# Delta rule in a two-block forward pass: steps 10 to 22 of each head moved by one slot

## The reference, cut to what matters

```
proj = h @ w_in                                   # q, k, v, z of the delta rule; q x3, k, v, z of the attention
qkv  = silu(causal_depthwise_conv(concat(aq, ak, av), conv_w))
a_strict = where(strict, beta * (k @ k.T) * decay, 0)
sol  = triangular_solve(a_strict, [v * beta, k * beta * exp(g)], unit_diagonal=True)   # u, w
v_new = u - w @ state
o     = (q * exp(g)) @ state + (q @ k.T * decay) @ v_new
state = state * exp(g_last) + (k * exp(g_last - g)).T @ v_new
```

## Time and profile before

| what | value |
|---|---|
| median of 3 runs | 2958.02 us (2957.57 to 2958.8) |
| profiled execution | 2963.54 us, its span 2961.7 us |
| mean granted TensorE clock | 0.994 of full speed |
| busy: TensorE, VectorE, ScalarE, GpSimd | 97%, 73%, 50%, 15% of the span |
| instructions | 50340 |

### The profile page before, as it was taken

How to read it: one execution, slowest core, us unless ns; L and a number is a source line. 1 busy time by engine, 2 the same in 40 slices (tenths; PEclk the granted TensorE clock), 3 DMA queues, 4 the chain that set the end, 5 groups by cost and what they waited for, 6 DMA issues and landing times.

```text
span 2961.7 us, 50340 instructions
## 1 busy us (share of the span) xinstructions
PE 2881.1 (97%) x16934; PEld 2502.1 (84%) x16934; DVE 2167.7 (73%) x3182; ACT 1480.9 (50%) x2124; POOL 454.5 (15%) x188
## 2 busy tenths in 40 slices
PE   7999999999999999999999999999999999999998
PEld 6888888888888888888887787788888888888887
DVE  6677777777679888888877998976787437465456
ACT  4454444454344444444445777765544444444443
POOL 0111101111000000000000000000003435545443
PEclk9999999999999999999999999999999999999999
DMA  6544444554568888788875455466684666767655
GB/s 220 169 148 152 157 149 158 161 160 168 159 205 297 306 300 317 289 298 317 302 255 186 164 171 171 164 206 221 230 324 157 198 206 229 252 227 242 205 185 178
DMA packets 199089, 636.93 MB, mean 215 GB/s; under 512 B 32312, under 2 KB 46776, under 8 KB 198208
## 3 DMA queue, kind: packets, MB, share of 16 engines
q1 hardware_dynamic: 165024, 601.92, 58.6%
q10 hardware_dynamic: 33952, 33.52, 3.6%
HBM read 619.61 MB, written 15.75 MB: 215 GB/s over the span
## 4 chain that ended last, share of the span: by engine, by line
PE 75%; DVE 10%; issue 6%; ACT 5%; DMA 3%; ACTq 0%; DVEq 0%; SPq 0%; POOL 0%; POOLq 0%
PE gemm L552 46%; PE gemm L557 23%; DVE wl L1569 3%; ACT wh L1008 3%; DMA Em<-E_scratch 2%; PE side L896 1%; DVE dT L1759 1%; DVE dW L1757 1%; DMA raw<-in_stream 0%; PE side L878 0%; DMA E_scratch<-dA 0%; PE side L578 0%; DVE xs L1658 0%; DVE ny L1644 0%; DVE t L2180 0%
## 5 line engine op out<-in xcount | busy, mean ns | idle before, releaser
L552 PE MATMUL gemm<-xs,wh 128*128 128x512 f32 x5120 | 1624.9, 399 | 28.9 <-DVE stage L1574 8.1
L1008 ACT ACTIVATE wh<-raw 128x1024 fp32r<-128x1024 f32 x939 | 983.2, 1058 | 949.1 <-PE gemm L557 816.2
L1569 DVE TENSOR_TENSOR wl<-raw,wh 128x1024 fp32r<-128x1024 f32 x811 | 1033.1, 1279 | 459.1 <-ACT wh L1008 436.9
L557 PEld LDWEIGHTS gemm<-xs,wl 128*128 128x128 f32 x5120 | 964.1, 188 | 215.8
L557 PE MATMUL gemm<-xs,wl 128*128 128x256 f32 x5120 | 1013.6, 279 | 0.0
L552 PEld LDWEIGHTS gemm<-xs,wh 128*128 128x128 f32 x5120 | 780.1, 189 | 60.6 <-issue 44.1
L552 PE MATMUL gemm<-hid,wh 128*128 128x512 f32 x2368 | 745.0, 396 | 8.9 <-DVE xacc L1601 2.3
L557 PEld LDWEIGHTS gemm<-hid,wl 128*128 128x128 f32 x2368 | 445.1, 188 | 101.3
L557 PE MATMUL gemm<-hid,wl 128*128 128x256 f32 x2368 | 467.4, 279 | 0.0
L1497 POOL TENSOR_TENSOR wl<-raw,wh 128x1024 fp32r<-128x1024 f32 x128 | 350.2, 2741 | 364.7 <-ACT wh L1008 360.4
L552 PEld LDWEIGHTS gemm<-hid,wh 128*128 128x128 f32 x2368 | 357.0, 188 | 12.5 <-issue 3.7
(11 more groups left out here) (393 smaller groups left out, 1804.2 us busy)
## 6 DMA issues: line engine op xcount, KB each, us to landing
raw<-in_stream SPq DMA_DIRECT2D x940, 512.0 KB, 4.1
ada_a<-in_ada SPq DMA_DIRECT2D x144, 512.0 KB, 5.1
ada_b<-in_ada SPq DMA_DIRECT2D x48, 512.0 KB, 5.1
stash<-stage ACTq DMA_DIRECT2D x12, 512.0 KB, 3.4
att<-stash ACTq DMA_DIRECT2D x8, 384.0 KB, 4.4
x<-in_x SPq DMA_DIRECT2D x4, 512.0 KB, 5.7
A_scratch<-gB ACTq DMA_DIRECT2D x8, 256.0 KB, 3.6
Em<-E_scratch ACTq DMA_DIRECT2D x8, 256.0 KB, 6.4
```

Source lines behind the costliest of these rows:

```text
L552: mm(G[n][:, :], wh[:, slot, at:at + P], rhs(sl * SLAB_K + k), start=sl == 0 and k == 0, stop=False, skip_group_check=True)
L557: op = mm(G[n][:, T:2 * T], wl[:, slot, at:at + P], rhs(sl * SLAB_K + k)[:, 0:T], start=False, stop=last, skip_group_check=True)
L1008: A(wh[:, slot, :], raw[:, slot, :], ACT.Copy).then_inc(hi_ready, 1)
L1569: tt(wl[:, slot, :], raw[:, slot, :], wh[:, slot, :].bitcast(F32), ALU.subtract).then_inc(lo_ready[slot], 1)
```

## The change

One line is edited. Steps 0 to 9 stay; steps 10 to 22 each stand one slot later. Steps that stood in odd slots now stand in even ones and the other way round.

```
     DELTA_AT = {slot: s for s, slot in enumerate(
-        (0, 2, 4, 5, 8, 9, 11, 15, 18, 20, 23, 24, 25, 26, 27, 28, 29, 31, 33, 35, 37, 39, 41))}
+        (0, 2, 4, 5, 8, 9, 11, 15, 18, 20, 24, 25, 26, 27, 28, 29, 30, 32, 34, 36, 38, 40, 42))}
     ATTN_AT = {1: 0, 6: 1, 9: 2, 12: 3, 33: 4, 37: 5, 40: 6, 43: 7}
```

## The result

The changed kernel takes 2963.40 us (median of 20 runs, 2959.31 to 2969.65) against 2959.12 us of the kernel before on the same chips (20 runs). The ratio is 1.0014 with a 95% interval of 1.0008 to 1.0020, so 4.1 us slower (2.4 to 5.9). The forecast was 2.6 us slower. The profiled execution took 2965.33 us with a span of 2963.5.

The account below looks back on a forecast made before the run. TensorE was taken as the bound, 75% of the chain of waits. A loss of 14.9 us less a gain of 12.3 made it 2.6 us slower than 2958.0: 2960.6 us, with 8 in 10 for 2952 to 2966.

Parts of the forecast that it names:

- The wait at Em: Step 10's matmuls (L682) wait for the load from E_scratch; moving them one slot later removes 10.4 us over 8 heads.
- the 0.16 that each wait hides: At step 10, each wait was taken as 0.16 us longer than its row shows, making 10.0 shown into 11.2 us.
- the gain term of 12.3: All gains in us: 10.4 from step 10's removed wait, 0.7 from its faster start, 1.2 at step 14.
- Sst behind the softmax: The state copy falls behind ScalarE's exponentials and the slab 20 split; step 19 stalls, costing 1.86 us per head, 14.9 total.
- Step 14's wait: Step 14 starts 0.06 us late behind VectorE's mask product; that and 0.11 for the standstill go in 7 heads: 1.2 us gained.
- The surcharge of a standstill: Products starting after TensorE stood still take 0.11 us longer; saved at step 10 in 6 heads (0.7 us), added at step 19.
- Step 16 at the group's end: Step 16 (slot 30) comes ahead of evacuating banks 2 and 3; 2 us available against 0.7 for its sum, so no cost.
- The other steps: Remaining moved steps, such as 11, 15 and 20 to 22, were expected to stay hidden behind other work, at no cost.
- the backlog rival: VectorE stays late after the state copy, so step 22 stalls 0.6 us per head, 5 us: 2965.6 us; chance 0.17.
- The Trainium skill's rule for a transfer's time: 2.0 us plus bytes over 436 GB/s gives 2.6 us for the Em load; rejected because the trace showed 6.4.
- The faster rival: The softmax does not get in the way and step 19 never stalls: 12.3 us faster, 2945.7 us; chance 0.13.

Follow-up runs that it names:

- tail_back: Changed kernel with steps 18 to 22 back in their old slots, steps 10 to 17 still moved: 2950.43 us, 10.7 us faster than before.
- tail_only: Kernel before with only steps 18 to 22 moved one slot later, steps 10 to 17 in their old slots: 2974.69 us, 12.1 us slower than before.
- exp_later: Changed kernel with ScalarE alone doing attention part 4's exponentials in slot 34, behind its split of slab 20: 2948.79 us, 11.3 us faster than before.
- step17_back: As `tail_back`, with step 17 also back in its old slot 31, directly behind step 16: 2954.79 us, 4.7 us faster than before.
- before_exp_later: Kernel before, steps in old slots, with ScalarE alone doing attention part 4's exponentials in slot 34: 2958.34 us, ratio 0.9994 to before.

## Why the prediction was right, point by point
The mechanism was right on both sides. That the sum came within 1.5 us of the result is in part luck: it is the difference of two terms of 12 and 15 us, and the runs that took them apart (`tail_back` 10.7 faster, `tail_only` 12.1 slower) know each to some 4 us only.

- **The wait at Em goes.** Right in kind: 10.0 to 0.9 us, shown again by `tail_back`. Two places were off. What is left is in two heads, but one of them is head 1 (step 10 shows 0.33 there). And the size: the four profiles with the old order of steps 10 to 17 show 10.0, 5.7, 8.7 and 6.6 us. With the 0.16 that each wait hides that is 11.3, 6.5, 9.8 and 7.4, on average 8.7, where the sum took 11.2 from the one profile at hand. That execution took 2963.54 us, near the slow end of the kernel's 20 runs (2955.0 to 2965.3). By these profiles the gain term of 12.3 was some 2.5 too large, and with 9.8 the sum gives 5.1 us slower; measured 4.1 (2.4 to 5.9). The 10.7 (7.1 to 14.2) of `tail_back` cannot tell 9.8 from 12.3.
- **Sst behind the softmax.** Right, link by link: 6.85 against 6.87 us from the attention product to step 19, 13.2 us of waits where 12 to 14 were named. TensorE asked 0.08 sooner than worked out, since step 18 took 0.36 (248.60 to 248.96) and not 0.44. `tail_only` shows the loss alone, 12.1 us against 14.9 forecast, within its interval; `exp_later` takes the named cause away and the wait is gone.
- **Step 14's wait.** Right: in head 1 of the changed kernel step 14 starts 1.47 us after the slot before it (234.84 to 236.31) and takes 0.81 (to 237.12), where it took 0.91, and it is so in all seven heads of the projection. No experiment tested it by itself.
- **The surcharge of a standstill.** Half right. It turns up at step 19: 0.92 (253.63 to 254.55), against 0.81 in the earlier trace rows. But it did not leave step 10 with the wait. Of the six heads (2 to 7) in which step 10 no longer waits, three still have it, with TensorE busy up to the product. TensorE and its weight loads (PEld) in the changed kernel, head 2 and then head 3:

```profile
314.72 0.39 PE L557 MATMUL gemm<-xs,wl 128*128 128x256 f32 x2
314.98 0.97 PEld L682 LDWEIGHTS side<-Em,gB 128*128 128x128 f32 x8
314.98 1.16 PE L682 MATMUL side<-Em,gB 128*128 128x128 f32 x8
```
```profile
402.29 0.97 PEld L682 LDWEIGHTS side<-Em,gB 128*128 128x128 f32 x8
402.40 1.05 PE L682 MATMUL side<-Em,gB 128*128 128x128 f32 x8
```

In head 3 the first weight load starts 0.11 ahead of the product, under the gemm, and the eight products hold TensorE for 0.81. In head 2 both start together, 0.26 behind the last gemm pair, and they hold it for 0.92. So the 0.11 comes with a first weight load that did not run ahead, whether TensorE stood still or not. That it waited for `Em` is read and not tested: the load of head 2 was issued at 308.39, and the median of 6.5 us to landing puts its end at about 314.9. The term of 0.7 us was worth about half in this profile; in the second one only two heads (6 and 7) still had the surcharge.

- **Step 16 at the group's end.** Its cost of nothing was right, its reasoning was not: I gave it 2 us against 0.7 for the sum and left out the evacuation and the split queued ahead. The margin in head 1 of the changed kernel is 0.8 us (sum ends 243.71, step 17 starts 244.51), and without the second slot `step17_back` pays for it.
- **The other steps.** No new wait at L738, L746 or L751 in the profile of the changed kernel; the backlog rival fell.
- **The Trainium skill's rule for a transfer's time**, as the prediction cites it, would have had the load land before TensorE asked, and the change cost its whole loss of 15 us. For this load it fell: the fastest of the old kernel's two profiles took 4.9 us, not 2.6, though no wait, as by the rule, was seen in the three heads of the second profile. The section is on GpSimd's path, and this load goes through ScalarE's queue, so no run here tests the rule where it was made for. The prediction's "6.4 in every head" is the median: the earlier trace rows have 6.3 to 7.2.
- **The faster rival** fell: the stall at step 19 is there in every head. Its 12 us could be had, though: `tail_back` and `exp_later` have 11. The changed kernel missed them by where one copy stood.

## What to carry to other kernels
When a step is moved to cover one wait, work out the place of every later step in each engine's written order, and above all whether it has passed another engine's work. Here 13 steps moved, 12 brought no new wait of TensorE, and one, a copy of 0.42 us, came to stand behind a chain of 6.4 us over three engines that the old order had kept off the path with 0.07 us to spare. A wait for a DMA should be sized over more than one execution, since a single profile can show it at its largest; the wait behind an engine's written order repeated to a tenth here.

## What the runs showed of the hardware that I had not expected
A wait of TensorE can cost more than its length. Waits of 3.1 us were followed by a granted clock of 0.50 to 0.57 over the next 4 us in six of eight cases, and a head took 90.1 to 91.9 us in those against 88.75 where the clock stayed (head 6). Keeping TensorE at work in the wait held the clock at 1.00 and brought every head to 88.4 to 88.7, what head 6 took without it. The Trainium skill (TensorE: Matmul & The Clock Gate, "Part 1: The HAM clock gate") says that the array falls to 1.2 GHz when it idles and returns with activity; the traces agree in both directions, but not in every case: two of the eight waits of 3.1 us left the clock at 1.00.

The kernel before had paid this once, unread by me: in head 5, behind the wait of 1.86 us, the clock was down, and this, not the wait alone, makes that head's 89.45 us; it is 2.3 above the other heads, and the wait only 0.7 longer than most:

```profile
573.70:575.80 2.10, 0.23 (x3) 0.04 (x2) 1.47 (x4) 1.06 (x1) 0.00 (x0) 1.00 0.91 331
575.80:578.90 3.10, 3.10 (x16) 2.76 (x17) 1.82 (x2) 0.00 (x0) 0.00 (x0) 0.70 0.22 87
578.90:581.00 2.10, 2.10 (x12) 2.06 (x12) 0.22 (x1) 0.00 (x0) 0.00 (x0) 0.63 0.51 113
```

The eight waits of some 1.66 us in the changed kernel, almost as long, kept 1.00 in every head, so the change's new waits add nothing of this. What the kernel before pays of it in some executions goes with the wait at Em; the sum has no term for it. The length alone does not decide. In `before_exp_later` (head 4) a wait of 1.87 us was followed by 0.57 over 4 us and a head of 89.31 us; in `tail_only` (head 3) one of 2.05 us was followed by 1.00. The lengths of the rows show it:

```profile
485.29 1.99 PE L682 MATMUL side<-Em,gB 128*128 128x128 f32 x8 [1.87 <-DMA Em<-E_scratch]
```
```profile
406.21 1.16 PE L682 MATMUL side<-Em,gB 128*128 128x128 f32 x8 [2.05 <-DMA Em<-E_scratch]
```

What decides between such cases was not settled.
